# Gate and up weights of every expert pair fetched in halves by rows, with three small reorderings beside it

## The chip, the cores and the metric

The kernel is one program on one core of a Trainium2 chip. The metric is the device time of one execution in microseconds; less is better. TensorE (PE) multiplies, VectorE (DVE) and ScalarE (ACT) move results out of the accumulator banks and do the elementwise work, GpSimd (POOL) does small side work, and SyncE (SP) issues the transfers from HBM. A weight reaches the PE only after a DMA has landed it in on-chip memory.

## The reference, cut to what matters

The reference runs two transformer blocks one behind the other, each with two layers, over 256 positions of width 1024 in float32. The change is in the second block, in the mixture of experts that closes each of its layers, and in the norm behind it:

```
def hier_moe(x, rg_w, rg_b, re_w, re_b, w_gate, w_up, w_down):
    ...                       # pick 1 group of 4, then 2 experts of its 8, for each token
    for g in range(N_GROUPS):
        h = silu(einsum('td,edf->tef', t, w_gate[g])) * einsum('td,edf->tef', t, w_up[g])
        y = y + einsum('tef,efd->td', h * gate[:, g, :, None], w_down[g])

for l in range(DEPTH):        # DEPTH = 2
    mix = hybrid_mixer(x, ...)
    x = layer_norm(ALPHA * x + mix, ln1_g[l], ln1_b[l])
    moe = hier_moe(x, ...)
    x = layer_norm(ALPHA * x + moe, ln2_g[l], ln2_b[l])
```

There are 32 experts with a hidden width of 256. Gate, up and down weights of one expert are 1 MB (1024 x 256 floats) each, so a layer reads 96 MB of expert weights.

## The kernel before

The experts are taken two at a time: sixteen pairs (duos) d = 0 to 15 a layer. The two experts of a pair run side by side on the two halves of the PE's columns, 64 columns each. At most 40 tokens are gathered for one expert in one pass; the program holds the code for more passes, but this input needs one (`npass`).

In a layer the order is: router matmuls, then DVE chooses the experts (`chosen`); five small matmuls L1798 to L1802 into the bank `ranks` count for every token how many earlier tokens chose the same expert (`before` is a strict triangle of ones, `ones` is all ones, `chosen` holds zeros and ones); DVE makes from the counts the one-hot matrices `pick`; then `moe_pass` runs the sixteen pairs. On the PE one pair is, in program order:

- `gate_up2(d)`, L1859: 8 row blocks k of the input times gate and up of both experts. The contraction over 1024 rows is done in 8 steps, so the first half needs only the weights of rows k = 0 to 3. It adds into one bank.
- a first part of the `gather` of tokens for a later group of pairs, L1818 (pairs 0 to 13 have some; pairs 14 and 15 have none). `gathers_in(d)` lists the parts that fall to pair d: two of them for pairs 1 to 9, one for pairs 10 to 13.
- `scatter(d - 1)`, L1899: the result of the pair before is put back onto the token rows, eight matmuls, two into each of four banks (`sc` 0 to 3, which gather the sum of all pairs).
- `turn_hidden(d)`, L1872: two transposes of the hidden values, which ACT then copies to the array `hT` (L2308).
- the second part of the gather if there is one, `turn_picks(d + 1)`, L1832, and `down2(d)`, L1885, which needs `hT` from ACT and the down weights.

In pairs 14 and 15, which gather nothing, the scatter is already cut: banks 0 to 2, then the transposes, then bank 3.

Weights. Even pairs use six slots of 1 MB in `ring`, odd pairs six slots in `high` and in free parts of `arena`. So the loads of pair d go into slots that pair d - 2 has read. SP issues them in program order (`expert_loads`, L1190); before each it waits until the PE's semaphore says that the slot's last reader is done. `halved(d)` says how gate and up are cut. Before the change it holds for pairs 0 to 3, 14 and 15: eight DMAs of 512 KB, four with the rows of k = 0 to 3 of both experts and then four with those of k = 4 to 7; the first four slots' worth is released in the middle of `gate_up2` (key `gh`), and the PE waits for each half when it comes to it. For pairs 4 to 13 gate and up are four DMAs of 1 MB, all are released at the end of `gate_up2`, and all four are waited for at its start. The down weights are always two DMAs of 1 MB. The partition's share of a row block lies in one piece in HBM: 8 KB in a whole load, 4 KB in a half. Behind pair 15 SP issues two parameter vectors for the last norm (L1194).

After the pairs, `add_scattered` (L3076) adds the four banks to the residual `H` with row sums, ACT squares the rows (L2338), POOL makes the reciprocal deviation (`rstd2`) with L3241 and L3244, and `second_norm` on DVE makes `centred` (L3088) and then the new `H` (L3095) for each of the two row tiles t. In the last layer SP stores `H` (L1229): tile 0 whole, tile 1 in two halves. In the first layer the PE's transposes of the next layer (`turn_stream`, L1568) start on it.

Of the kernel before, what the change touches and what calls it, by code (L numbers as in the profile page):

```python
# [25 lines left out]
BF16 = mybir.dt.bfloat16  # L26
# [9 lines left out]
TT = SEQ // P  # L36
# [64 lines left out]
DUOS = GROUPS * EXPERTS // 2  # L101
# [3 lines left out]
HALVED = 4  # L105
LAST_HALVED = DUOS - 2
# [132 lines left out]

def halved(d):  # L240

    return d < HALVED or d >= LAST_HALVED


def unit_slot(key):
# [100 lines left out]
def build(nc, src, out, debug=None):  # L346
# [7 lines left out]
    with ctx:  # L354
# [37 lines left out]
        ones = sb("ones", [P, P])  # L392
# [91 lines left out]
        before = carve(P)  # L484
# [82 lines left out]
        chosen_flat = carve(TT * GROUPS * EXPERTS)  # L567
# [667 lines left out]
        def _(pe):  # L1235
# [294 lines left out]
            def fill(mm, key):  # L1530
                mm.then_inc(filled[banks2[key]], 1)
# [173 lines left out]
            for l in range(LAYERS):  # L1705
# [19 lines left out]
                for i in range(4):  # L1725
                    t, half = divmod(i, 2)
                    acc = claim2(("uq", i), l)
# [66 lines left out]
                keep_running(bank2(("ranks", 0)), 4)  # L1794
                pe.wait_ge(chosen_done.sem, chosen_done.at(l, 1))
                acc = bank2(("ranks", 0))
                of_tile = chosen_flat.rearrange("p (t n) -> p t n", t=TT)
                nc.tensor.matmul(acc[:, 0:32], before, of_tile[:, 0, :], start=True, stop=True)  # L1798
                nc.tensor.matmul(acc[:, 32:64], before, of_tile[:, 1, :], start=True, stop=False)
                nc.tensor.matmul(acc[:, 32:64], ones[:], of_tile[:, 0, :], start=False, stop=True)  # L1800
                nc.tensor.matmul(acc[:, 64:96], ones[:], of_tile[:, 0, :], start=True, stop=False)
                fill(nc.tensor.matmul(acc[:, 64:96], ones[:], of_tile[:, 1, :], start=False, stop=True), ("ranks", 0))  # L1802

                def moe_pass(pass_):
                    lp = l * PASSES + pass_
# [61 lines left out]
                    def turn_hidden(d):  # L1867

                        pe.wait_ge(h2_done.sem, h2_done.at(lp, d + 1))
                        acc = bank2(("hT", 0, d))  # L1870
                        for j in range(2):
                            mm = nc.tensor.transpose(acc[:, j * P:(j + 1) * P], hh[:, d % 2, j::2], ident[:])  # L1872
                        fill_p(mm, "hT", d)
# [43 lines left out]
                    for d in range(DUOS):  # L1917
                        if first and d == DUOS // 2:
                            wait_apart(pe, npass_done.sem, npass_done.at(l, 1))
                            passes = pe.value_load(npass[0:1, 0:1], min_val=1, max_val=PASSES)  # L1920
                        gate_up2(d)
                        todo = gathers_in(d)
                        if todo:
                            pe.wait_ge(pT_in.sem, pT_in.at(lp, d + 1))
                            for at in todo[0:5 if d == 0 else 1]:
                                gather(*at)
                            if d == 1:
                                for n in range(1, 5):
                                    evicted(1, n)
                            if d > 0:  # L1930
                                scatter(d - 1)
                            turn_hidden(d)
                            for at in todo[5 if d == 0 else 1:]:
                                gather(*at)
                        else:
                            scatter(d - 1, 0, 2)
                            turn_hidden(d)
                            scatter(d - 1, 3, 3)
                        if d < DUOS - 1:
                            if todo:  # L1940
                                evicted(*todo[0])
                            else:
                                pe.wait_ge(pT_in.sem, pT_in.at(lp, d + 1))
                            turn_picks(d + 1)
                        down2(d)
# [402 lines left out]
        def _(dve):  # L2348
# [311 lines left out]
            for l in range(LAYERS):  # L2660
# [423 lines left out]
                def second_norm():  # L3084

                    dve.wait_ge(mean_in.sem, mean_in.at(l, TT))
                    for t in range(TT):
                        nc.vector.scalar_tensor_tensor(out=centred[:, t, :], in0=H[:, t, :], scalar=less_mean[:, t:t + 1],  # L3088
                                                       in1=lng[:, 0, :], op0=ALU.add,
                                                       op1=ALU.mult).then_inc(centred_in.sem, 1)  # L3090
                    for t in range(TT):
                        dve.wait_ge(centred_in.sem, centred_in.at(l, t + 1))
                        wait_apart(dve, rstd_done.sem, rstd_done.at(l, 2 + t + 1))
                        for cols in OUT_PARTS[t] if l == LAYERS - 1 else (slice(0, D),):
                            nc.vector.scalar_tensor_tensor(out=H[:, t, cols], in0=centred[:, t, cols],  # L3095
                                                           scalar=rstd2[:, t:t + 1], in1=lng[:, 1, cols], op0=ALU.mult,
                                                           op1=ALU.add).then_inc(x_ready.sem, 1)
                    if l < LAYERS - 1:
                        head_low(l + 1)
# [171 lines left out]
```

## Time and profile before

| What | Value |
|---|---|
| median of 3 runs | 1680.45 us (1679.74 to 1682.97) |
| profiled execution, its own time | 1677.06 us |
| its span, first to last instruction | 1675.3 us |
| TensorE busy | 1644.5 us, 98% of the span |
| granted TensorE clock, mean | 0.996 |
| expert pairs of layer 1 and of layer 2 in the span | about 1025 to 1256 us, 1432 to 1664 us |
| DMA in these stretches | 421 GB/s, engines' busy share 1.01 |

The profiled execution was 3.4 us faster than the median of the runs. All times in the rows are counted from the start of its span; 1.8 us of its time lie outside the span. A PE share of 98% says only that a matmul was nearly always under way; where two things run at their limit side by side, as the PE and the DMA do in the expert stretches, the landing time of a load beside the start of the matmul that reads it tells which is nearer to deciding.

### The profile page before, as it was taken

The numbers are of one execution on the slowest core, as the hardware profiler recorded it, in microseconds if no ns is written. First come the engines' busy times: TensorE is split into PE (matmuls) and PEld (weight loads), VectorE is DVE, ScalarE is ACT, GpSimd is POOL, SyncE is SP. The second block draws the span as 40 slices with busy tenths as digits, with TensorE's granted clock in tenths as the row PEclk, the third lists the DMA queues.
The fourth block names the chain that finished last, engine by engine and source line by source line (L and its number), as shares of the span: only waits on it lengthen the run. The fifth ranks groups of instructions, "written<-read, shape, count | busy, mean of one in ns | idle before, by whom it ended". The sixth has DMA issues, their size and how long they took to land. (4 is left out here: it accounts for less than half of the span.)

```text
span 1675.3 us, 23546 instructions
## 1 busy us (share of the span) xinstructions
PE 1644.5 (98%) x9413; PEld 1248.6 (75%) x9413; DVE 856.2 (51%) x1420; ACT 651.0 (39%) x920; POOL 173.7 (10%) x242
## 2 busy tenths in 40 slices
PE   9999999999999999999999999999998999999997
PEld 7888879999798887999988976444448887544443
DVE  6566564444646556544456867322126785532123
ACT  5455444343445454434345453111114464211111
POOL 2020001111102000111111040000002023000000
PEclk9999999999999999999999999999999999999998
DMA  9544545553654455555456646999996636699996
GB/s 323 184 138 151 176 151 188 188 182 119 238 184 133 149 176 176 169 183 189 137 185 194 189 141 226 407 421 421 421 398 199 193 127 243 229 420 421 422 417 259
DMA packets 158587, 396.61 MB, mean 237 GB/s; under 512 B 20752, under 2 KB 85264, under 8 KB 140048
## 3 DMA queue, kind: packets, MB, share of 16 engines
q1 hardware_dynamic: 158480, 395.18, 65.1%
q8 instruction: 67, 1.10, 0.3%
q14 instruction: 40, 0.33, 0.1%
HBM read 394.10 MB, written 1.05 MB: 236 GB/s over the span
## 5 line engine op out<-in xcount | busy, mean ns | idle before, releaser
L946 PE MATMUL ps<-split,split 128*128 128x256 f32 (+3 forms) x1872 | 631.5, 337 | 1.0 <-DVE split L939 0.7
L950 PE MATMUL ps<-split,split 128*128 128x256 f32 (+3 forms) x1872 | 627.7, 335 | 0.1
L947 PE MATMUL ps<-split,split 128*128 128x256 f32 (+3 forms) x1872 | 623.6, 333 | 0.0
L924 DVE TENSOR_TENSOR split<-ring,split 128x2048 fp32r<-128x2048 f32 x136 | 312.6, 2305 | 253.9 <-ACT split L917 253.8
L946 PEld LDWEIGHTS ps<-split,split 128*128 128x128 f32 x1872 | 351.6, 188 | 36.1 <-issue 2.1
L950 PEld LDWEIGHTS ps<-split,split 128*128 128x128 f32 x1872 | 351.8, 188 | 35.7 <-DVE split L2386 1.2
L947 PEld LDWEIGHTS ps<-split,split 128*128 128x128 f32 x1872 | 352.9, 189 | 33.0 <-issue 0.5
L917 ACT ACTIVATE split<-ring 128x2048 fp32r<-128x2048 f32 x136 | 260.3, 1915 | 277.8 <-PE ps L950 268.2
L1859 PE MATMUL ps<-ring,arena 128*64 128x512 f32 x464 | 105.8, 592 | 0.0
L3037 DVE SCALAR_TENSOR_TENSOR arena<-arena,ps 128x256 f32<-128x256 f32 x32 | 15.4, 481 | 167.0 <-ACT arena L2303 131.3
L1859 PE MATMUL ps<-arena 128*64 128x512 f32 x288 | 99.3, 593 | 0.0
L939 DVE TENSOR_TENSOR split<-ring,split 128x1536 fp32r<-128x1536 f32 (+3 forms) x44 | 80.7, 1851 | 25.5 <-ACT split L933 25.3
L3049 DVE TENSOR_TENSOR split<-ps,split 128x512 fp32r<-128x512 f32 x64 | 44.3, 692 | 95.6 <-ACT split L2310 95.6
L1859 PE MATMUL ps<-high,arena 128*64 128x512 f32 x256 | 92.0, 592 | 0.0
L2303 ACT ACTIVATE arena<-ps 128x256 f32<-128x256 f32 x32 | 12.3, 385 | 200.1 <-PE ps L1859 200.1
L933 ACT ACTIVATE split<-ring 128x1536 fp32r<-128x1536 f32 (+3 forms) x44 | 67.7, 1547 | 49.4 <-PE ps L950 46.5
L1859 PEld LDWEIGHTS ps<-ring,arena 128*64 128x64 f32 x464 | 36.2, 137 | 62.1 <-issue 62.1
L2310 ACT ACTIVATE split<-ps 128x512 fp32r<-128x512 f32 x64 | 38.2, 597 | 106.7 <-PE ps L1885 106.7
L1859 PEld LDWEIGHTS ps<-high,arena 128*64 128x64 f32 x256 | 29.2, 137 | 57.3 <-issue 57.3
L1899 PE MATMUL ps<-split,split 128*128 128x512 f32 x240 | 62.3, 399 | 0.0
L1818 PEld LDWEIGHTS ps<-split,split 128*128 128x128 f32 x320 | 43.9, 190 | 24.5 <-issue 24.5
L1885 PE MATMUL ps<-ring,arena 128*64 128x512 f32 x256 | 58.5, 598 | 1.5 <-ACT arena L2308 1.5
(260 smaller groups left out, 1700.4 us busy)
## 6 DMA issues: line engine op xcount, KB each, us to landing
ring<-in_w_in SPq DMA_DIRECT2D x52, 1024.0 KB, 5.1
ring<-in_w_gate_up SPq DMA_DIRECT2D x44, 1024.0 KB, 5.3
ring<-in_expert_w_down SPq DMA_DIRECT2D x32, 1024.0 KB, 13.2
ring<-in_w_down SPq DMA_DIRECT2D x22, 1024.0 KB, 5.0
ring<-in_w_in SPq DMA_DIRECT2D x28, 768.0 KB, 4.6
ring<-in_expert_w_gate SPq DMA_DIRECT2D x20, 1024.0 KB, 12.0
ring<-in_expert_w_up SPq DMA_DIRECT2D x20, 1024.0 KB, 14.1
arena<-in_expert_w_down SPq DMA_DIRECT2D x16, 1024.0 KB, 14.6
```

The costliest lines, as they stand in the source:

```text
L917: nc.scalar.activation(split(high[:, n % HIGH, :]), ring[:, units[key], :], ACT.Copy).then_inc(high_done.sem, 1)
L924: nc.vector.tensor_tensor(split(slot), slot, split(high[:, n % HIGH, :]), ALU.subtract).then_inc(low_done.sem, 1)
L933: nc.scalar.activation(split(high[:, n % HIGH, 0:used(key)]), ring[:, units2[key], 0:used(key)], ACT.Copy).then_inc(high2_done.sem, 1)
L939: nc.vector.tensor_tensor(split(slot), slot, split(high[:, n % HIGH, 0:used(split2[n])]), ALU.subtract).then_inc(low2_done.sem, 1)
L946: nc.tensor.matmul(acc, sh, mh, start=start, stop=False)
L947: nc.tensor.matmul(acc, *second, start=False, stop=False)
L950: return nc.tensor.matmul(acc, *third, start=False, stop=stop)
L1818: mm = nc.tensor.matmul(acc[:, j * SEQ:j * SEQ + XG_cols[g]].rearrange("p (e n) -> p e n", n=TAKEN_SLOTS), moe_split((H_high, H_low)[part] ...
L1859: mm = nc.tensor.matmul(acc[i * SLOTS:(i + 1) * SLOTS, :].rearrange("p (s n) -> p s n", s=2), XG[g % 2][:, at:at + SLOTS], w_[:, :, k % w_ ...
L1885: mm = nc.tensor.matmul(bank2(("yg", 0, d, half))[i * SLOTS:(i + 1) * SLOTS, :], hT[:, d % 2, j * P + i * SLOTS:j * P + (i + 1) * SLOTS], ...
L1899: mm = nc.tensor.matmul(bank2(("sc", 0, i)), moe_split(pickT[:, d % 2, (TT - 1 - t) * P:(TT - t) * P]), moe_split(Y[:, part, half * 512:(h ...
L3049: nc.vector.tensor_tensor(moe_split(Y[:, 1, cols]), acc, moe_split(Y[:, 0, cols]), ALU.subtract).then_inc(y_low.sem, 1)
```

## The change

There are four edits. (1) `halved(d)` now holds for every pair, so that pairs 4 to 13 fetch gate and up in eight loads of 512 KB like the others, with two release points and two waits. (2) In the pairs with one gather part, 10 to 13, the scatter into bank 3 comes behind the transposes. (3) The five ranks matmuls read the upper 16 bits of their float32 operands as bfloat16 (zeros and ones are exact in them), with a step of two. (4) `second_norm` makes `centred` and `H` of tile 0 and then those of tile 1, where before both `centred` came first.

```
 def halved(d):
-    return d < HALVED or d >= LAST_HALVED
+    return d < DUOS
...
-                of_tile = chosen_flat.rearrange("p (t n) -> p t n", t=TT)
-                nc.tensor.matmul(acc[:, 0:32], before, of_tile[:, 0, :], start=True, stop=True)
+                all_, earlier = (m.bitcast(BF16)[:, 1::2] for m in (ones[:], before))
+                of_tile = chosen_flat.bitcast(BF16)[:, 1::2].rearrange("p (t n) -> p t n", t=TT)
+                nc.tensor.matmul(acc[:, 0:32], earlier, of_tile[:, 0, :], start=True, stop=True)
...
                             if d > 0:
-                                scatter(d - 1)
+                                scatter(d - 1, 0, 3 if len(todo) > 1 else 2)
                             turn_hidden(d)
+                            if d > 0 and len(todo) == 1:
+                                scatter(d - 1, 3, 3)
...
                         nc.vector.scalar_tensor_tensor(out=centred[:, t, :], ...)
-                    for t in range(TT):
                         dve.wait_ge(centred_in.sem, centred_in.at(l, t + 1))
                         wait_apart(dve, rstd_done.sem, rstd_done.at(l, 2 + t + 1))
```

On SP, the gate and up loads of one odd pair (5) before the change; `filled0` is the semaphore of the bank that gate and up add into, `filled3` that of the down product:

```order
L1190 DMA high<-in_expert_w_gate 128x2048 [waits filled0]
L1190 DMA high<-in_expert_w_up 128x2048 [waits filled0]
L1190 DMA arena<-in_expert_w_gate 128x2048 [waits filled0]
L1190 DMA arena<-in_expert_w_up 128x2048 [waits filled0]
L1190 DMA high<-in_expert_w_down 128x2048 [waits filled3]
L1190 DMA arena<-in_expert_w_down 128x2048 [waits filled3]
```

The same pair on SP after the change:

```order
L1190 DMA high<-in_expert_w_gate 128x1024 [waits filled0]
L1190 DMA high<-in_expert_w_up 128x1024 [waits filled0]
L1190 DMA high<-in_expert_w_gate 128x1024 [waits filled0]
L1190 DMA high<-in_expert_w_up 128x1024 [waits filled0]
L1190 DMA arena<-in_expert_w_gate 128x1024 [waits filled0]
L1190 DMA arena<-in_expert_w_up 128x1024 [waits filled0]
L1190 DMA arena<-in_expert_w_gate 128x1024 [waits filled0]
L1190 DMA arena<-in_expert_w_up 128x1024 [waits filled0]
L1190 DMA high<-in_expert_w_down 128x2048 [waits filled3]
L1190 DMA arena<-in_expert_w_down 128x2048 [waits filled3]
```

Six loads of a pair have become ten for the same bytes; `high` now holds the first row half of both experts, where before it held the whole gate and up of the first expert.

On the PE, pair 10 of a layer before the change, from the scatter to the down product:

```order
L1899 MATMUL ps<-split_51,split_58 128x512 [waits pT_in,y_low]
L1899 MATMUL ps<-split_51,split_58 128x512 x7
L1872 MATMUL ps<-ident,arena 128x128 [waits h2_done]
L1872 MATMUL ps<-ident,arena 128x128
L1832 MATMUL ps<-split_57 128x192 [waits xg_act]
L1832 MATMUL ps<-split_57 128x192
L1885 MATMUL ps<-ring,arena 64x512 [waits hT_in,landed5,landed4]
L1885 MATMUL ps<-ring,arena 64x512 x7
```

The same place after the change, where all line numbers are one higher:

```order
L1900 MATMUL ps<-split_51,split_58 128x512 [waits pT_in,y_low]
L1900 MATMUL ps<-split_51,split_58 128x512 x5
L1873 MATMUL ps<-ident,arena 128x128 [waits h2_done]
L1873 MATMUL ps<-ident,arena 128x128
L1900 MATMUL ps<-split_51,split_58 128x512 [waits pT_in,y_low]
L1900 MATMUL ps<-split_51,split_58 128x512
L1833 MATMUL ps<-split_57 128x192 [waits xg_act]
L1833 MATMUL ps<-split_57 128x192
L1886 MATMUL ps<-ring,arena 64x512 [waits hT_in,landed5,landed4]
L1886 MATMUL ps<-ring,arena 64x512 x7
```

Two of the eight scatter matmuls now stand between the transposes and the down product, which waits for ACT's copy of the transposes (`hT_in`).

On DVE, the second norm of the last layer before the change:

```order
L3088 SCALAR_TENSOR_TENSOR arena<-H,arena 128x1024 [waits mean_in]
L3088 SCALAR_TENSOR_TENSOR arena<-H,arena 128x1024
L3095 SCALAR_TENSOR_TENSOR H<-arena 128x1024 [waits centred_in,rstd_done]
L3095 SCALAR_TENSOR_TENSOR H<-arena 128x512 [waits centred_in,rstd_done]
L3095 SCALAR_TENSOR_TENSOR H<-arena 128x512
```

And after it:

```order
L3091 SCALAR_TENSOR_TENSOR arena<-H,arena 128x1024 [waits mean_in]
L3097 SCALAR_TENSOR_TENSOR H<-arena 128x1024 [waits centred_in,rstd_done]
L3091 SCALAR_TENSOR_TENSOR arena<-H,arena 128x1024
L3097 SCALAR_TENSOR_TENSOR H<-arena 128x512 [waits centred_in,rstd_done]
L3097 SCALAR_TENSOR_TENSOR H<-arena 128x512
```

The `centred` of tile 1 has moved behind the wait for the deviation of tile 0.

## Rows read from the trace of the kernel before

**Rows 1.** The page's busy times, and the DMA's busy tenths in 40 slices.
```profile
PE 1644.5 (98%) x9413; PEld 1248.6 (75%) x9413; DVE 856.2 (51%) x1420; ACT 651.0 (39%) x920; POOL 173.7 (10%) x242
DMA  9544545553654455555456646999996636699996
```

**Rows 2.** Windows: stretch, length, busy times (count), PEclk, DMA share, GB/s.
```profile
1464.00:1472.00 8.00, 8.00 (x39) 2.54 (x35) 3.25 (x3) 0.63 (x2) 0.00 (x0) 1.00 1.04 423
1563.00:1623.00 60.00, 58.91 (x290) 28.10 (x288) 12.76 (x29) 10.79 (x22) 0.00 (x0) 1.00 1.01 421
1623.00:1655.00 32.00, 31.64 (x153) 14.06 (x149) 5.83 (x14) 3.93 (x8) 0.00 (x0) 1.00 1.02 412
```

**Rows 3.** Timeline of SP: last gate/up loads of pairs 4, 13, 14, 15; layer 1's 15.
```profile
1472.38 0.43 SPq L1190 DMA_DIRECT2D ring<-in_expert_w_up  x1
1600.59 0.43 SPq L1190 DMA_DIRECT2D arena<-in_expert_w_up  x1
1617.81 2.13 SPq L1190 DMA_DIRECT2D ring<-in_expert_w_up  x1
1631.81 5.19 SPq L1190 DMA_DIRECT2D arena<-in_expert_w_up  x1
...
1225.95 2.20 SPq L1190 DMA_DIRECT2D arena<-in_expert_w_up  x1
```

**Rows 4.** DMA view of these five issues, same order; last column us to landing.
```profile
ring<-in_expert_w_up SPq DMA_DIRECT2D x1, 1024.0 KB, 14.0
arena<-in_expert_w_up SPq DMA_DIRECT2D x1, 1024.0 KB, 20.0
ring<-in_expert_w_up SPq DMA_DIRECT2D x1, 512.0 KB, 18.0
arena<-in_expert_w_up SPq DMA_DIRECT2D x1, 512.0 KB, 19.2
...
arena<-in_expert_w_up SPq DMA_DIRECT2D x1, 512.0 KB, 18.0
```

**Rows 5.** Timeline of PE: both halves of pair 15 (layer 2), second half (layer 1).
```profile
1648.00 3.60 PE L1859 MATMUL ps<-high,arena 128*64 128x512 f32 x16
1651.43 3.60 PE L1859 MATMUL ps<-arena 128*64 128x512 f32 x16
...
1244.45 3.60 PE L1859 MATMUL ps<-arena 128*64 128x512 f32 x16
```

**Rows 6.** PE before the down product: one case of pair 12, then all of L1885.
```profile
1602.97 0.61 PE L1885 MATMUL ps<-high,arena 128*64 128x512 f32 x1 [0.36 <-ACT arena L2308]
...
  ACT arena L2308: 2.9, 8
```

**Rows 7.** Timeline of DVE around the ranks matmuls of layer 2.
```profile
1429.39 1.22 DVE L2879 TENSOR_TENSOR split<-arena,split 128x1024 fp32r<-128x1024 f32 x1
1430.94 0.23 DVE L2959 SCALAR_TENSOR_TENSOR arena<-ps,arena 128x64 f32<-128x64 f32 x1 [0.33 <-PE ps L1802]
```

**Rows 8.** Timeline of the last norm; last row: POOL's same step L3237 over the program.
```profile
1665.80 2.48 DVE L3088 SCALAR_TENSOR_TENSOR arena<-H,arena 128x1024 f32<-128x1024 f32 x2
1666.03 1.46 POOL L3244 TENSOR_TENSOR arena<-arena,minus_half 128x1 f32<-128x1 f32 x1 [0.18 <-POOL arena L3241]
1667.58 0.75 POOL L3241 TENSOR_SCALAR arena<-arena 128x1 f32<-128x1 f32 x1
...
1668.51 1.37 POOL L3244 TENSOR_TENSOR arena<-arena,minus_half 128x1 f32<-128x1 f32 x1 [0.18 <-POOL arena L3241]
1670.01 1.41 DVE L3095 SCALAR_TENSOR_TENSOR H<-arena 128x512 f32<-128x512 f32 x2 [0.54 <-POOL arena L3244]
L3237 POOL TENSOR_TENSOR arena<-arena,minus_half x4: 555/562/570, 1009.6 to 1419.6; 128x1 f32<-128x1 f32 x4
```

**Rows 9.** Windows of PE between the layers: busy (count), PEclk, DMA share, GB/s.
```profile
1261.00:1262.00 1.00, 0.17 (x1) 1.00 1.08 380
1263.00:1264.00 1.00, 0.10 (x1) 0.69 0.13 48
```

More of the change, by code:

```diff
@@ L1796, in _ @@
                 acc = bank2(("ranks", 0))
-                of_tile = chosen_flat.rearrange("p (t n) -> p t n", t=TT)
-                nc.tensor.matmul(acc[:, 0:32], before, of_tile[:, 0, :], start=True, stop=True)
[L1799 to L1802, printed above, removed]
+                all_, earlier = (m.bitcast(BF16)[:, 1::2] for m in (ones[:], before))
+                of_tile = chosen_flat.bitcast(BF16)[:, 1::2].rearrange("p (t n) -> p t n", t=TT)
+                nc.tensor.matmul(acc[:, 0:32], earlier, of_tile[:, 0, :], start=True, stop=True)
+                nc.tensor.matmul(acc[:, 32:64], earlier, of_tile[:, 1, :], start=True, stop=False)
+                nc.tensor.matmul(acc[:, 32:64], all_, of_tile[:, 0, :], start=False, stop=True)
+                nc.tensor.matmul(acc[:, 64:96], all_, of_tile[:, 0, :], start=True, stop=False)
+                fill(nc.tensor.matmul(acc[:, 64:96], all_, of_tile[:, 1, :], start=False, stop=True), ("ranks", 0))
                 def moe_pass(pass_):
```

## The prediction

> **What bounds the kernel now.** I read the page first: the PE is busy for 98% of the span, and the DMA engines stand at nine tenths or more only in two stretches, the expert pairs of the two layers of the second block [rows 1]. All edits lie in these stretches or at their ends, so I asked the windows view for them. In the middle of layer 2's stretch the PE and the DMA both run without a gap: clock 1.00, 421 GB/s at a DMA share of 1.01 [rows 2]. Two things at their limit side by side means that landing times decide. So next I took single issues of SP, and from the DMA view the time from each to its landing [rows 3, 4]. Issue plus latency gives the landing of the last gate or up load of a pair: pair 4 at 1472.38 + 14.0 = 1486.4; pair 13 at 1600.59 + 20.0 = 1620.6; pair 14 at 1617.81 + 18.0 = 1635.8; pair 15 at 1631.81 + 19.2 = 1651.0. The matmuls that read the last one start at 1651.43 [rows 5]. That is 0.4 us behind the landing. In layer 1 the same load lands at 1225.95 + 18.0 = 1243.95 and is read at 1244.45: 0.5 us behind. So the PE still sets the time, but the weight stream has caught up with it to less than half a microsecond in both layers. The latency grows from 14.0 to 19.2 us, so the stream falls steadily behind the releases of its slots: there are always loads waiting in the queue, and what decides when a late load lands is the stream's rate and not when SP may issue it.
>
> **(1) Halves for pairs 4 to 13.** Ten pairs in each of two layers go from six loads to ten, for the same 6 MB. What it removes: the wait for all four megabytes at the start of a pair (each such pair may now start with half of them), and 3.4 us of waiting before half of the slots are released (1651.43 - 1648.00, the length of a half [rows 5]). Neither gains anything here: pair 13, the tightest whole pair, does not wait before its matmuls (the windows show a PE busy for 58.91 of 60 us with four 0.36 us pauses, which belong to edit 2 [rows 2, 6]), and an earlier issue only lengthens a queue that is never empty. At SP four more issues of 0.43 us a pair [rows 3] are 1.7 us in a pair of some 14, beside a queue that is never empty; nothing on the PE waits for SP but the loads themselves. That two issues take 2.13 and 5.19 us [rows 3] shows that SP is made to wait when some ten loads are under way; more loads mean more of that, but again with a full queue behind it.
>
> What it costs is the stream's rate. The last loads of pair 4 and of pair 13 are nine pairs apart, of whole loads: (1620.6 - 1486.4) / 9 = 14.91 us a pair. From pair 13 to 14 and from 14 to 15, which are already halved, it is 15.2 and 15.2 us. So a halved pair takes 0.30 us longer. The windows say the same: 421 GB/s in the stretch of whole loads, 412 in that of halves, and 6.29 MB a pair at these rates are 14.94 and 15.27 us, a difference of 0.33. But there is a row against it: 423 GB/s in 1464 to 1472, when the halves of pair 3 were being moved with a short queue [rows 2]. The bounds are therefore 0 and 0.4 us a pair; I take 0.30, by the two steps with a long queue, since from pair 4 on the queue is long. Over ten pairs the stream is 3.0 us later at pair 15. The PE had 0.42 us to spare there in layer 2 and 0.50 in layer 1. It ends later by 3.0 - 0.42 = 2.6 and 3.0 - 0.50 = 2.5 us, whatever the PE gains before that. The down weights come behind with the same delay and are not late first. Sum: +5.1 us; at the bounds -0.9 (0 a pair) and +7.1 (0.4 a pair).
>
> The Trainium skill ("DMA: Bandwidth & Descriptors", section Bandwidth, under Measured) advises batching transfers to 1 MiB or more for at least three quarters of the peak rate, and gives for one transfer a fit of about 2.0 us plus the bytes at 436 GB/s. By an estimate from that page a pair of whole loads would take 6 x (2.0 + 2.4) = 26 us one behind the other and a halved one 8 x (2.0 + 1.2) + 2 x (2.0 + 2.4) = 34. The rule points the same way as this edit's cost, but the trace doesn't bear out its size: a halved pair took 15.2 us, so the fixed part is hidden when many loads are queued.
>
> **(2) The last bank of the scatter.** In pairs 10 to 13 the down product waits for ACT's copy of the transposes: 0.36 us in one pair, 2.9 us in eight [rows 6]. Two scatter matmuls now stand in that gap and come out of the time ahead of it, so the pause goes: up to 1.45 us a layer. What is late next is the stream. With (1) the PE then stands waiting for the weights of pairs 13 to 15 all the more, and the gain is already in the sum above: the end of the stretch is the landing of pair 15 plus a fixed rest. Value 0; if the stream didn't bind, -2.9 for both layers.
>
> **(3) Ranks.** Fewer, shorter passes on the PE. Behind them DVE starts L2959 after a pause of 0.33 us for L1802, but until 1429.39 + 1.22 = 1430.61 it is busy with L2879, which stands ahead in its queue [rows 7]. That covers all but 0.33 us; I take -0.3 a layer. What follows (picks, gather, pair 0, the release of the first slots, so the stream too) moves with it. Sum -0.6, bounds -0.7 and 0.
>
> **(4) The second norm.** Before, DVE made both `centred` in 2.48 us (1665.80 to 1668.28), by when POOL had the deviation of tile 0 (1666.03 + 1.46 = 1667.49). Then tile 0, a pause of 0.54 us, and tile 1's two halves from 1670.01 [rows 8]. After, DVE ends the first `centred` at 1667.04, waits until about 1667.6, writes tile 0 until 1668.9, makes the second `centred` until 1670.1, and only then starts the halves. If POOL's two steps for tile 1 fit in beside it, the halves start at 1670.2 to 1670.3. POOL's step takes 1.37 to 1.46 us here and 0.56 elsewhere with DVE idle, and each ends 0.4 us after a DVE instruction has ended [rows 8]. If L3241 gets behind tile 0's write, POOL is done at 1670.5 and the halves start at 1670.6. So +0.3 at the end of the program, bounds -0.2 and +0.6. At the end of layer 1 the next layer's transposes begin in the window 1263 to 1264, behind a pause of the PE [rows 9] that the view puts down to no other engine's result; I count 0 there.
>
> The Trainium skill ("SBUF — State Buffer", section SBUF: two separate sides) says that a DVE instruction with two inputs in SBUF and a GpSimd one that reads SBUF exclude each other for a whole instruction. The 1.46 against 0.56 us agrees. Without such a lock POOL would be done by 1666.6, the halves could start at 1669.7, and the edit would be worth -0.3.
>
> **The sum.** +5.1 + 0 - 0.6 + 0.3 = +4.8 us. On the profiled execution's own time that is 1677.06 + 4.8 = 1681.9. The median of the runs is 3.4 us above that execution; the same difference on 1680.45 gives 1685.2, and I say 1685.
>
> **Rivals.**
> *The halves cost nothing.* The stream keeps 14.91 us a pair, as the 423 GB/s row allows; the two slow steps then came from the ten-deep queue and not from 4 KB pieces. The stream still sets the end, 0.42 and 0.50 us earlier than now: -0.9 - 0.6 + 0.3 = -1.2, so 1679.3. Against it: both steps, and the window beside them.
> *The PE sets the end and the pauses are gained.* This ends on the other side. It needs pair 15's last load 1.0 us earlier than now in both layers, for instance because releases 3.4 us earlier let the stream run ahead in the first pairs. Place: pairs 10 to 13. Price: -2.9 - 0.6 + 0.3 = -3.2, so 1677.3. It decides from a halved pair of 14.81 us or less. For it: pair 14 to 15 has no pause with this very order. Against it: the queue is never empty behind pair 2.
> *The clock falls in the new waits.* Between the layers the PE did nearly nothing from 1261.2 to the end of the window 1263 to 1264, in which its granted clock fell to 0.69 [rows 9], from 2.4 GHz towards 1.2. The longest wait for a load could be the whole 2.6 us that the stream is late at pair 15. If that is enough, the rest of a half (3.43 us) doubles: about +3 a layer, 1691. Against it: the 2.6 us will mostly be spread over the waits of pairs 13, 14 and 15, with matmuls between.
>
> **How the numbers follow.** Two runs of this kernel can be told apart from about 0.2% on, 3.4 us: slower is above 1683.8, faster below 1677.1. Forecast (a cost of 0.15 to 0.4 us a pair): 0.60, and it lies above 1683.8 from a cost of 0.23 on, so 0.45 slower and 0.15 the same. No cost: 0.20, the same. PE sets the end: 0.14, on the border, 0.10 faster and 0.04 the same. Clock: 0.06, slower. That gives faster 0.11, same 0.38, slower 0.51; 0.02 goes from slower to faster for what no row shows. The forecast's own range is 1682 to 1688. The range for eight in ten takes in the no-cost case and half of the PE case below and leaves the clock out above: 1677.4 to 1688.5.
>
> **What would show it.** Right: the last gate/up loads of pairs 5 to 15 land 15.2 us apart, windows of 412 GB/s all along, idle time of the PE in front of L1860 in pairs 13 to 15 of some 1 to 2 us each put down to a DMA, and no pause before L1886. Wrong on (1): 14.9 us steps, 421 GB/s. Wrong on (3): L2962 (the old L2959) no earlier against the router. Wrong on (4): the last halves start less than 4.2 us behind the first `centred`. A stretch in which the PE never waits for a load would overturn the forecast as a whole.

## The result

The changed kernel takes 1683.77 us (median of 20 runs, 1681.35 to 1686.52) against 1679.56 us of the kernel before (20 runs, 1676.58 to 1682.97). The ratio is 1.0027, 95% interval [1.0021, 1.0034]: 4.5 us slower by the ratio (the two medians lie 4.2 us apart), where the sum of the prediction said +4.8.

The two profiled executions are 1677.06 us (span 1675.3) before and 1682.08 us (span 1680.3) after. The same events of both, side by side in time order:

| from, to | before | after | what the stretch adds |
|---|---|---|---|
| start to the choice of experts, layer 1 (nothing changed yet) | 1022.24 | 1023.05 | +0.8 |
| to pair 0's first gate/up matmul | 1029.11 | 1029.87 | -0.05 |
| to the second half of pair 15 | 1244.45 | 1248.12 | +2.9 |
| to the first `centred` of the norm | 1258.83 | 1262.54 | 0.0 |
| to layer 2's first product (L946) | 1268.25 | 1270.78 | -1.2 |
| to the choice of experts, layer 2 | 1429.18 | 1431.74 | 0.0 |
| to pair 0's first gate/up matmul | 1436.05 | 1438.19 | -0.4 |
| to the second half of pair 15 | 1651.43 | 1656.09 | +2.5 |
| to the first `centred` of the norm | 1665.80 | 1670.50 | 0.0 |
| to the end of the span | 1675.3 | 1680.3 | +0.3 |

The time is lost in the two expert stretches. The page of the kernel after, its busy times and the DMA's rows (they answer to [rows 1]; the GB/s row has the same 40 slices):

```profile
PE 1644.6 (98%) x9403; PEld 1242.4 (74%) x9403; DVE 856.3 (51%) x1420; ACT 650.7 (39%) x920; POOL 172.1 (10%) x242
DMA  8544545553754455555366546999996637699996
GB/s 319 182 142 151 175 151 190 186 185 115 244 182 131 145 177 174 176 180 195 125 200 195 172 158 232 398 414 413 413 400 202 196 120 259 234 412 413 413 412 259
DMA packets 170107, 396.61 MB, mean 236 GB/s; under 512 B 22032, under 2 KB 86544, under 8 KB 161808
```

PE's busy time is that of before to 0.1 us, with ten matmuls fewer (the ranks). The rate tells the rest: 412 to 414 GB/s in the slices that lie inside an expert stretch, for the same 396.61 MB. The windows of layer 2's stretch (stretch, length, busy times with counts of PE, PEld, DVE, ACT, POOL; granted clock, DMA share, GB/s) answer to [rows 2]:

```profile
1464.00:1472.00 8.00, 8.00 (x40) 2.73 (x38) 3.95 (x7) 1.19 (x2) 0.00 (x0) 1.00 1.03 413
1503.00:1563.00 60.00, 60.00 (x294) 29.11 (x294) 14.26 (x32) 11.31 (x22) 0.00 (x0) 1.00 1.02 413
1563.00:1623.00 60.00, 60.00 (x296) 26.99 (x294) 13.10 (x33) 11.38 (x23) 0.00 (x0) 1.00 1.02 413
1623.00:1655.00 32.00, 29.65 (x140) 12.53 (x136) 6.02 (x15) 3.92 (x8) 0.00 (x0) 1.00 1.02 414
```

421 GB/s has become 413 in the long windows, and PE, which before paused 1.09 us in 1563 to 1623, now pauses there not at all: it stands only at the very end. Where the last gate/up loads of pairs 4, 13, 14 and 15 land is again SP's issue plus the time to landing from the DMA view (they answer to [rows 3, 4]; all are 512 KB now, and the last of each block is layer 1's pair 15):

```profile
1475.51 0.43 SPq L1190 DMA_DIRECT2D ring<-in_expert_w_up  x1
1608.14 2.20 SPq L1190 DMA_DIRECT2D arena<-in_expert_w_up  x1
1622.71 2.20 SPq L1190 DMA_DIRECT2D ring<-in_expert_w_up  x1
1636.77 5.19 SPq L1190 DMA_DIRECT2D arena<-in_expert_w_up  x1
...
1230.22 2.19 SPq L1190 DMA_DIRECT2D arena<-in_expert_w_up  x1
```

```profile
ring<-in_expert_w_up SPq DMA_DIRECT2D x1, 512.0 KB, 13.4
arena<-in_expert_w_up SPq DMA_DIRECT2D x1, 512.0 KB, 17.5
ring<-in_expert_w_up SPq DMA_DIRECT2D x1, 512.0 KB, 18.0
arena<-in_expert_w_up SPq DMA_DIRECT2D x1, 512.0 KB, 19.2
...
arena<-in_expert_w_up SPq DMA_DIRECT2D x1, 512.0 KB, 17.8
```

Pair 4 lands at 1488.9, pair 13 at 1625.6, pair 14 at 1640.7, pair 15 at 1656.0: (1656.0 - 1488.9) / 11 = 15.19 us a pair, where the whole loads of before took 14.91. Pair 15 landed at 1651.0 before. Less the 2.15 us by which this execution already was later at pair 0 (1438.19 - 1436.05), the stream is 2.8 us late in layer 2, and 4.07 - 0.76 = 3.3 us in layer 1 (1248.02 against 1243.95).

The timeline of PE shows where these microseconds are waited for (each row 16 matmuls, one half of a pair; in brackets the idle time before it). It answers to [rows 5]:

```profile
1625.73 3.65 PE L1860 MATMUL ps<-arena 128*64 128x512 f32 x16 [0.53 <-DMA arena<-in_expert_w_up]
1640.89 3.65 PE L1860 MATMUL ps<-ring,arena 128*64 128x512 f32 x16 [1.10 <-DMA ring<-in_expert_w_up]
1650.99 3.65 PE L1860 MATMUL ps<-high,arena 128*64 128x512 f32 x16 [0.37 <-SPq L1208]
1656.09 3.65 PE L1860 MATMUL ps<-arena 128*64 128x512 f32 x16 [1.44 <-SPq L1208]
```

All waits of PE for expert weights, over both layers (engine, line, what it waited for: us in total, times, longest):

```profile
PE ps L1860 <- SPq L1208: 3.6, 4, 1.4
PE ps L1860 <- DMA ring<-in_expert_w_up: 2.2, 2, 1.1
PE ps L1860 <- DMA arena<-in_expert_w_up: 1.4, 2, 0.9
```

The four waits put down to "SPq L1208" are the same kind as the others: L1208 is an instruction of SP that happened to end near, but the second half of pair 15 starts at 1656.09, 0.1 us behind a landing at 1655.97. So there are eight waits, 7.2 us. The 2.9 us in which PE used to wait for ACT before the down product [rows 6] are gone from this view, so PE stands only some 4.3 us longer than before (7.2 - 2.9).

### The profile page after: what moved, and what is told of

The parts are those of the page before. It is cut to its first block and busy times, and to the rows that moved or that the text cites. A ratio compares the mean times of both kernels' runs of the same rounds, so it can differ in the third digit from the quotient of the medians.

```text
span 1680.3 us, 23614 instructions
## 1 busy us (share of the span) xinstructions
PE 1644.6 (98%) x9403; PEld 1242.4 (74%) x9403; DVE 856.3 (51%) x1420; ACT 650.7 (39%) x920; POOL 172.1 (10%) x242
## 2 busy tenths in 40 slices
DMA packets 170107, 396.61 MB, mean 236 GB/s; under 512 B 22032, under 2 KB 86544, under 8 KB 161808
## 5 line engine op out<-in xcount | busy, mean ns | idle before, releaser
L946 PE MATMUL ps<-split,split 128*128 128x256 f32 (+3 forms) x1872 | 631.3, 337 | 1.2 <-DVE split L939 0.7
L946 PEld LDWEIGHTS ps<-split,split 128*128 128x128 f32 x1872 | 351.5, 188 | 36.3 <-issue 2.1
L1860 PE MATMUL ps<-arena 128*64 128x512 f32 x288 | 65.2, 594 | 4.3 <-SPq L1208 2.9
L1886 PE MATMUL ps<-ring,arena 128*64 128x512 f32 x256 | 58.5, 598 | 0.1
L1860 PE MATMUL ps<-high,arena 128*64 128x512 f32 x256 | 57.8, 593 | 0.8 <-SPq L1208 0.8
L1886 PE MATMUL ps<-high,arena 128*64 128x512 f32 x128 | 58.3, 598 | 0.2
```

The source lines that it names most:

```text
L946: nc.tensor.matmul(acc, sh, mh, start=start, stop=False)
L1860: mm = nc.tensor.matmul(acc[i * SLOTS:(i + 1) * SLOTS, :].rearrange("p (s n) -> p s n", s=2), XG[g % 2][:, at:at + SLOTS], w_[:, :, k % w_ ...
L1886: mm = nc.tensor.matmul(bank2(("yg", 0, d, half))[i * SLOTS:(i + 1) * SLOTS, :], hT[:, d % 2, j * P + i * SLOTS:j * P + (i + 1) * SLOTS], ...
```

## The experiments

Each was compared with the kernel before on the same chip; the times are medians. "Before" measured 1678.6 to 1679.4 us in these comparisons.

**The halves alone.**

```
-    return d < HALVED or d >= LAST_HALVED
+    return d < DUOS
```

> Only the halving of gate and up for pairs 4 to 13; scatter, ranks and second norm as before. Theory (the weight stream runs at 413 GB/s in place of 421 and sets the end of each layer's pairs): in the profile of the whole change the stretch from the first matmul of pair 0 to the second half of pair 15 grew by 2.9 and 2.5 us, so about +5.4 us here; steps of 15.2 us a pair, and PE waits for the loads of pairs 13 to 15 that are shorter than in the whole change (3.2 to 4.0 us a layer there), since the PE keeps its four pauses of 0.36 us before the down product: about 2.5 us a layer. Rival (the halving is harmless and the slowdown came from the three other edits): 0 us within 1.

Measured: 1684.46 us, ratio 1.0031 [1.002, 1.0041], +5.2 us. The waits of PE:

```profile
PE ps L1859 <- SPq L1208: 3.6, 4, 1.4
PE ps L1885 <- ACT arena L2308: 2.9, 8, 0.4
PE ps L1859 <- DMA ring<-in_expert_w_up: 1.3, 1, 1.3
```

The whole loss is edit 1's. The stretch from pair 0 to the second half of pair 15 grew by 3.7 and 2.4 us. Here PE keeps its pauses before the down product, and waits for loads 4.9 us instead of 7.2: take the pauses away and the load waits grow by nearly as much.

**The other three edits alone.** The changed kernel with `halved(d)` as before.

> The three other edits without the halving: scatter's last bank, ranks, second norm. Theory (the whole-load stream at 421 GB/s sets the end as soon as the PE gains more than 0.42 to 0.50 us a layer): -0.9 (not -2.9) from the scatter, -0.4 to -0.8 from the ranks, +0.3 from the norm, so -1.2 us, and PE waits of about 1 us a layer at pairs 12 to 15. Rival (the PE sets the end, the pauses are gained whole): -3.2 us and no wait for a load.

Measured: 1678.64 us, ratio 0.9993 [0.9983, 1.0003], -1.2 us with an interval of +-1.7. Its rows:

```profile
1503.00:1563.00 60.00, 60.00 (x292) 28.79 (x292) 14.43 (x33) 10.80 (x22) 0.00 (x0) 1.00 1.01 421
PE ps L1860 <- DMA arena<-in_expert_w_up: 1.8, 2, 0.9
PE ps L1860 <- DMA ring<-in_expert_w_up: 0.8, 1, 0.8
PE ps L1860 <- SPq L1208: 0.2, 1, 0.2
```

421 GB/s again, and no pause before the down product. Even so PE now waits 2.8 us for loads: the 2.9 us that edit 2 takes out come back as waits, up to the slack of 0.4 to 0.5 us a layer. +5.2 and -1.2 give +4.0 with an uncertainty of some 2.5 us, and the whole change measured +4.5 +- 1.1: the parts add up within that.

**Less to load.** Two kernels: before, and after, each with only half of the down weights of pairs 4 and 5 loaded, 2.1 MB a layer less (these two pairs compute with stale rows; the instructions of the engines stay).

```
+LIGHT = (4, 5)
+                if name == "down" and key[2] in LIGHT:
+                    return w[:, 0:1, :]
```

> The kernel before, with only the first half of the down weights of pairs 4 and 5 loaded (2.1 MB a layer less to move; the rest of those weights is stale). Theory (in the kernel before the PE sets the end, by 0.4 us): the last loads land 5 us earlier and the time stays the same within 1 us. Rival (the stream already sets it): -5 us or more.

> The whole change, with the same 2.1 MB a layer of down weights left out. Theory: the stream is 5 us earlier and out of the way, the waits of 3.2 and 4.0 us before L1860 disappear, and the edits to the scatter and the ranks show their full worth: -7 to -8 us against the change, which is -3 against the kernel before. Rival (the waits come from elsewhere, from SP's issue or the release of slots, and not from bytes): they stay, and the time moves by less than 2 us.

Measured: the lighter before 1678.5 us, 0.9995 [0.9986, 1.0005]; the lighter after 1674.97 us, 0.9973 [0.9962, 0.9984]. The lighter after has one row of load waits left, the lighter before none:

```profile
PE ps L1865 <- SPq L1213: 1.1, 2, 0.8
```

This is the plainest of the experiments. 4.2 MB less in the program are 10 us of the stream at 413 GB/s. In before they buy nothing that can be told from zero (at most 0.0014 of 1679, 2.4 us). In after they buy 1.0027 - 0.9973 = 0.0054, 9 us, where 7 to 8 were expected. So in after the weights set the end of both stretches, and in before PE did, with the stream close behind. The profiles say the same: from pair 0 to the second half of pair 15 PE took 215.3 us in each layer of the lighter before, as in before, and 214.6 and 214.1 us in the lighter after, where after took 218.3 and 217.9.

Two things were not as expected. In the lighter before pair 15 did not land 5 us earlier: PE's second half began 2.2 and 2.3 us behind the landing, where before it was 0.5 and 0.4, so the load came only some 1.8 us earlier. The run still tells the two theories apart, but with 1.8 us a layer and not 5. And in the lighter after PE still waits 0.8 and 0.3 us at pair 15. With the stream mostly out of the way the change is worth 0.9973 - 0.9995, about -3.7 us with an uncertainty of some 2.4, which fits the price of the rival "the PE sets the end and the pauses are gained" (-3.2).

**Pieces or DMAs, first try.** Halving does two things: 4 KB pieces in place of 8 KB, and twice as many DMAs. To keep the 8 KB pieces and double the DMAs, the whole loads of pairs 4 to 13 were issued as two DMAs of 64 partitions each.

```
+                if name != "down" and not halved(key[2]):
+                    return w[64 * key[4]:64 * key[4] + 64]
```

> Before, with each whole gate and up load of pairs 4 to 13 issued as two DMAs of 64 partitions each: the same number of DMAs and the same 512 KB a DMA as after's halves, but each partition's piece stays 8 KB as before; PE still waits for the whole load. Theory A (the shorter pieces of 4 KB cost the stream its 2%): the stream stays at about 421 GB/s and 14.9 us a pair, and the time is that of before within 1 us. Theory B (the number of DMAs, or SP's issuing, costs it): the stream falls to 413 GB/s and 15.2 us a pair as in after, and the time is 4 to 5 us over before. Anything under 413 GB/s would say that DMAs over half the partitions are a cost of their own.

Measured: 1918.28 us, ratio 1.1422 [1.1407, 1.1438]. Neither theory; a DMA over half of the partitions is a cost of its own, and so large that this run says nothing on the question. Layer 2's pairs run from 1548 us to the end here, and the pairs with cut loads fill these two windows:

```profile
1683.00:1743.00 60.00, 34.21 (x136) 14.93 (x136) 6.71 (x15) 5.16 (x10) 0.00 (x0) 0.76 1.02 236
1743.00:1803.00 60.00, 36.05 (x144) 15.56 (x146) 5.54 (x13) 5.40 (x11) 0.00 (x0) 0.76 1.02 247
```

The stream fell to 236 to 247 GB/s, down weights included, at a DMA share of 1.02. PE waited 97.8 + 87.3 us for up loads, up to 12.2 us at a time, and in these windows its granted clock was 0.76, so it also worked more slowly between the waits.

**Pieces or DMAs, second try.** Here the number of DMAs and their 1 MB stay, and only the landing place is laid out as the halves are, so that each partition's 8 KB land as two pieces of 4 KB.

```
-            return slots.rearrange("p s (k n) -> p s k n", k=KT)
+            return slots.rearrange("p h (s k n) -> p h s k n", s=2, k=KT // 2)
...
+                if name != "down" and not halved(key[2]):
+                    return w.rearrange("p (h k) n -> p h k n", h=2)
```

> Before, with each whole gate and up load of pairs 4 to 13 still one DMA of 1 MB over 128 partitions, but laid into SBUF as the halves are (rows 0 to 3 of gate and of up in one slot, rows 4 to 7 in the next), so that each partition's 8 KB land as two pieces of 4 KB. PE still waits for the whole load. Theory A (the shorter pieces cost the stream its 2%): about 413 GB/s, 15.2 us a pair, and 3 to 6 us over before, since the waits at the end of a layer come as in the run with the halves alone (4.9 us of waits, plus those for whole loads). Theory B (the number of DMAs of 128 partitions, their start and end costs, is what costs it): 421 GB/s, 14.9 us a pair, and within 1 us of before.

Measured: 1684.99 us, ratio 1.0032 [1.002, 1.0044], +5.4 us.

```profile
1503.00:1563.00 60.00, 60.00 (x291) 28.08 (x288) 13.74 (x30) 11.10 (x22) 0.00 (x0) 1.00 1.02 413
1563.00:1623.00 60.00, 58.06 (x284) 28.23 (x283) 11.89 (x28) 10.43 (x22) 0.00 (x0) 1.00 1.02 413
DMA packets 168827, 396.61 MB, mean 236 GB/s; under 512 B 20752, under 2 KB 85264, under 8 KB 160528
```

Theory A: 413 GB/s with the old number of DMAs, and the stretch from pair 0 to the second half of pair 15 is 218.3 and 217.9 us, as in after. The last gate/up load of pair 4 lands at 1491.4 and that of pair 13 at 1628.1, 15.19 us a pair, as in after. The packets say what was doubled: 168827 is 10240 more than before's 158587, 128 for each of the 80 split loads. After has 11520 more, 144 for each: 128 pieces and 16 more. Those 16 and the extra issue cost nothing that shows. In HBM the two pieces of this run still lie together; in after they are fetched apart, at the same rate.

**Scatter and ranks alone** (edits 2 and 3, the second norm as before).

> Edits 2 and 3 alone (scatter's last bank behind the turn, ranks in BF16); loads and the second norm as before. The kernel without the halves but with the second norm measured 0.9993 of before. Theory (terms add): the ranks give 0.3 us a layer, the lost pause before the hidden activation lets the last two pairs' chain end up to 0.1 us earlier, and the second norm's +0.3 is not there: about 1.1 us under before, 0.9993 or a little less. Rival (the norm's order is worth nothing or a gain): the same as the run with all three edits, 0.9993, or more. The stretch from the last norm's first write to the last H should be 5.6 us as before, not 5.9.

Measured: 1677.62 us, ratio 0.9995 [0.9985, 1.0005]. The point lies 0.3 us from that of the three edits and the intervals cover both theories, so the time settles nothing on the norm's order. The profile does: from the start of the first `centred` to the end of the last `H` it is 5.6 us here as before (1666.86 to 1672.49), and 5.9 in after.

**Pair 3 whole as well**, with edits 2 and 3: the opposite direction of edit 1.

```
-HALVED = 4
+HALVED = 3
```

> Edits 2 and 3 as in the run beside it, and pair 3 loaded whole instead of in halves, the opposite direction of edit 1. Theory (each pair in halves costs the stream 0.30 us): the stream ends 0.3 us earlier in each layer; its slack at the end of a layer is 0.4 to 0.5 us, so pair 15 is waited for no more and little of it is given to the end: 0 to 0.6 us under the run with edits 2 and 3 alone. Rival (the halves of pair 3 are needed, since the stream has not filled its lead there): PE waits for pair 3's whole gate and up, 1 to 3 us a layer, and the time is 1 to 5 us over it.

Measured: 1676.39 us, ratio 0.9983 [0.9974, 0.9992], some 2.9 us under before: the fastest of all that ran with the whole work, and faster than both kernels. PE waits 1.5 us, twice, both before pair 13, and none of it for pair 3:

```profile
PE ps L1860 <- DMA arena<-in_expert_w_up: 1.5, 2, 0.9
```

By the ratios it is 2.0 us below the run with edits 2 and 3, by the medians 1.2, more than the 0 to 0.6 expected; the two intervals overlap, so against that run the times alone don't settle it. The profiles give the direction: pair 15's last load lands 215.02 and 214.39 us behind the start of pair 0 in the two layers, without this edit 215.55 and 214.94. That is 0.5 us a layer earlier, where 0.3 was expected.

**Pair 14 whole too**, on top of that (`LAST_HALVED = DUOS - 1`).

> The kernel with edits 2 and 3 and pair 3 whole, and now pair 14 whole too. By that kernel's trace, pair 14's first matmul begins at 1634.7 us and its last load lands at 1635.9: whole, it waits for it, about 1.2 us less the 0.3 that the stream gains, so 0.9 us a layer, and pair 15's second half, which began 0.2 us after its landing, gives nothing back. Theory (the end of the layer needs the halves): 1.5 to 2.5 us over that kernel, near before's time. Rival (the stream alone sets the end): 0.3 us a layer earlier, 0.6 us under it.

Measured: 1677.68 us, ratio 0.999 [0.9981, 0.9999], about 1.2 us over the kernel without it, a little less than expected; again the intervals overlap. The wait is where and as large as expected, 0.9 us before pair 14 in each layer:

```profile
PE ps L1860 <- DMA ring<-in_expert_w_up: 1.7, 2, 0.9
PE ps L1860 <- DMA arena<-in_expert_w_up: 0.7, 1, 0.7
```

So by the profiles the halves have a use where PE arrives before the whole load has landed, and they cost rate everywhere. That pair 14 is better in halves is read from these waits; the times of the last two runs don't prove it.

## Why the prediction was right, step by step

**What bounds the kernel.** Right. "PE still sets the time, but the stream has caught up to less than half a microsecond" is what the lighter loads show: nothing to gain by them in before, 9 us in after.

**(1) Halves.** Right in mechanism and size. 0.30 us a pair was forecast, 15.19 - 14.91 = 0.28 measured in layer 2. In layer 1 the mean step was 15.29: nine steps were 15.2, and two single ones 15.6 and 15.8. Such single long steps, up to 16.4 us, stand in most of the other profiles too, at changing places; their cause is open. The stretch grew by 2.9 us in layer 1 where +2.5 was forecast, in layer 2 by 2.5 where +2.6 was. The sum of the term was +5.1, the run with it alone gave +5.2. The choice between the two kinds of rows was the right one: the 423 GB/s of 1464 to 1472 [rows 2], which spoke for "the halves cost nothing", does not come back in after, where the same window has 413. A window of 8 us holds parts of a few loads only; the steps between landings, nine pairs apart, were the better measure. The second short-piece run shows that the cause is the length of the pieces; the prediction named it only in a rival and could not have told it from the number of DMAs. One reading was off and changed nothing: the window 1563 to 1623 holds three of the four 0.36 us pauses and not four (60 - 58.91 = 1.09). The waits of "1 to 2 us each" came as eight of 0.4 to 1.4 us, half of them put down to SP and not to a DMA. The fit of 2.0 us plus the bytes at 436 GB/s stands in the Trainium skill ("DMA: Bandwidth & Descriptors") in the section Anatomy of one DMA — SWDGE (gpsimd) path, for transfers that GpSimd issues. Here SyncE issues them, so the 26 and 34 us worked out from it are not a test of that page.

**(2) Scatter's last bank.** The forecast of no gain holds: the pauses before L1886 are gone, and the time comes back as waits for weights. Where the stream binds less, the gain is there, -3.7 us in the lighter pair of kernels, the ranks and the norm included.

**(3) Ranks.** -0.6 was the sum, and -0.45 came of it, unevenly. In layer 2 L2962 starts 1.35 us behind L2942, before 1.76: -0.4, all of the 0.33 us pause and a little more. In layer 1 only -0.05. The timeline of DVE, layer 1 and then layer 2 (it answers to [rows 7]):

```profile
1023.26 1.22 DVE L2882 TENSOR_TENSOR split<-arena,split 128x1024 fp32r<-128x1024 f32 x1
1024.76 0.23 DVE L2962 SCALAR_TENSOR_TENSOR arena<-ps,arena 128x64 f32<-128x64 f32 x1 [0.28 <-PE ps L1803]
...
1431.95 1.22 DVE L2882 TENSOR_TENSOR split<-arena,split 128x1024 fp32r<-128x1024 f32 x1
1433.09 0.22 DVE L2962 SCALAR_TENSOR_TENSOR arena<-ps,arena 128x64 f32<-128x64 f32 x1
```

The cause in layer 1 was the clock. Twelve filler matmuls (L1259) stand ahead of the ranks on the PE in both layers and in both kernels. They take 2.76 us at the full clock, and are done before the experts are chosen. In layer 1 of this execution they took 4.44, and the ranks began 1.3 us behind the start of L2942, where in layer 2 it was 0.35:

```profile
1020.09 4.44 PE L1259 MATMUL ps<-ones 128*128 128x512 bf16 x12
1022.00:1024.00 2.00, 2.00 (x7) 0.66 (x5) 1.86 (x11) 0.00 (x0) 0.00 (x0) 0.53 1.00 406
```

The granted clock was 0.53 there, near the lower level of 1.2 GHz, ahead of the first changed matmul, though the PE was busy all the time. It fell at this place in three other profiles too, the one with short pieces among them, whose PE program is that of before, so the change isn't the cause. Two other profiles with edits 2 and 3 kept the full clock at this place (the run of those two edits alone and that with pair 14 whole), and there L2962 starts 1.35 and 1.34 us behind L2942 in layer 1 as well. So at the full clock the edit is worth 0.4 us in each layer, 0.8 in all and just outside the bounds of -0.7 and 0, a little over the 0.33 us of the pause, since L2962 now starts just before L2882 has ended; in layer 1 of the profiled execution it was lost by bad luck.

**(4) The second norm.** +0.3 forecast, +0.28 measured in the profile, by the order of events that was written down. The timeline of the last norm answers to [rows 8]:

```profile
1670.50 1.28 DVE L3091 SCALAR_TENSOR_TENSOR arena<-H,arena 128x1024 f32<-128x1024 f32 x1
1670.73 1.46 POOL L3246 TENSOR_TENSOR arena<-arena,minus_half 128x1 f32<-128x1 f32 x1 [0.18 <-POOL arena L3243]
1672.29 0.19 POOL L3243 TENSOR_SCALAR arena<-arena 128x1 f32<-128x1 f32 x1
1672.33 1.28 DVE L3097 SCALAR_TENSOR_TENSOR H<-arena 128x1024 f32<-128x1024 f32 x1 [0.54 <-POOL arena L3246]
1672.66 1.36 POOL L3246 TENSOR_TENSOR arena<-arena,minus_half 128x1 f32<-128x1 f32 x1 [0.18 <-POOL arena L3243]
1673.53 1.28 DVE L3091 SCALAR_TENSOR_TENSOR arena<-H,arena 128x1024 f32<-128x1024 f32 x1
1674.98 1.42 DVE L3097 SCALAR_TENSOR_TENSOR H<-arena 128x512 f32<-128x512 f32 x2 [0.18 <-DVE arena L3091]
```

DVE pauses 0.54 us before the first `H`, where before it used that time for the second `centred`. POOL's L3243 got in during this pause, 0.04 us before `H` starts. Its L3246 then ran beside two long DVE instructions, took 1.36 us and ended 0.4 us after one of them, as the steps in [rows 8] do. DVE's last halves wait for no POOL result, but for DVE's own `centred`, which is now in front of them. That agrees with the rule of the Trainium skill ("SBUF — State Buffer", section SBUF: two separate sides) on the two engines excluding each other; no run here changed POOL's part, so the rule itself wasn't tested.

**What the sum did not have.** The profiled execution of after gained 1.2 us between the layers; the PE's first eight transposes there (L1568) took 1.16 us, before 1.97. Before, the clock fell while PE stood idle there [rows 9]; after, it didn't:

```profile
1262.00:1266.00 4.00, 2.84 (x14) 1.07 (x11) 3.39 (x6) 3.77 (x7) 3.15 (x4) 1.00 1.06 390
1266.00:1270.00 4.00, 2.25 (x15) 1.74 (x16) 3.43 (x3) 1.42 (x1) 0.05 (x1) 1.00 0.23 56
```

This is no effect of the change. Of the nine other profiles, three kept 1.00 as well (the halves alone, the lighter before, pair 14 whole), and the six others fell to between 0.51 and 0.64 in windows of 4 us, as before did (0.67), the lighter after among them, which has all four edits. It is one part of the spread of some 6 us between runs of one kernel, and it stood by luck against the +0.8 us by which this execution was late before the first changed instruction.

**The rivals.** "The halves cost nothing" fell with the windows. "The PE sets the end" fell, but its price (-3.2) fits what was measured with less to load (-3.7). "The clock falls in the new waits" fell: the longest wait in after is 1.4 us, the granted clock is 1.00 in all windows of the stretch (the 2.4 GHz level), and the 16 matmuls behind a wait last 3.65 us where before they lasted 3.60. With waits of up to 12.2 us it did fall, in the run with DMAs over 64 partitions (0.76). The chances in the prediction add up to 0.10, 0.39 and 0.51 for its cases, where it writes 0.11, 0.38 and 0.51; nothing hangs on it.

## What to carry to other kernels

When two resources run side by side without a gap, measure the slack in landing times (issue plus latency against the first reader), not in busy shares, and price a change of the load pattern by the steps between landings many loads apart. Here splitting a load helped only at the place where its reader arrives before the whole has landed, and everywhere else it cost the rate of the stream; so look for these places in the trace and leave the loads between them whole. A pause taken out of the engine ahead of such a stream comes back as a wait for it: first give the stream room, as the version with pair 3 whole does, then remove pauses.

## What the runs showed of the hardware

- The length of the contiguous piece of a partition set the rate of a full queue, and the number of DMAs did not: 8 KB pieces 420 to 421 GB/s, 4 KB pieces 413, at DMA shares of 1.01 and 1.02; the same 413 with 1 MB DMAs and with 512 KB DMAs. A pair in halves has 512 more pieces, 32 for each of 16 DMA engines, and takes 0.28 us more: about 9 ns a piece, an estimate from these steps.
- With the gate and up loads in DMAs over 64 of the 128 partitions the stream ran at 236 to 247 GB/s, against 421 over all of them with the same 8 KB pieces, at a DMA share of 1.02, and the kernel was 14% slower. No run shows why.
- The Trainium skill ("DMA: Bandwidth & Descriptors", section Bandwidth) advises transfers of 1 MiB or more for at least three quarters of the peak rate, from measurements of transfers that GpSimd issued. Here, with some ten loads of SyncE queued, no run shows a loss by the size of the DMA: 512 KB loads and 1 MB loads with equal pieces ran alike, at 413 GB/s.
- The clock between the layers: behind the same kind of idle stretch of PE, of some 3 us, four profiles kept 1.00 and seven fell to between 0.51 and 0.67 (windows of 4 us), for about 1.2 us of time. In layer 1 of after it also fell without an idle stretch, to 0.53 in 1022 to 1024, where the PE had just run its router matmuls of 36 columns and then the fillers; in before the same work kept 1.00. What decides it stays open.
